# Hybrid attention and expert block: values as weights in two column halves, result kept turned

## The reference

```python
xn = rms_norm(h, attn_norm_w)
q_a, k_a, v_a, q_b, k_b, v_b, g_a, g_b = split(xn @ w_in)
# y_a: sliding window (128), 8 heads of 64 over 2 key heads, QK-norm, ALiBi, a sink per head
probs = softmax(concat([scores, sink]))[..., :-1];  y_a = probs @ v_a
# y_b: stick-breaking, 8 heads of 64, strictly causal
between = cumsum(log_keep, reverse=True) - log_keep
weights = where(strict, exp(log_beta + between), 0);  y_b = weights @ v_b
merged = sigmoid(g_a) * (y_a @ w_proj_swa) + sigmoid(g_b) * (y_b @ w_proj_sb)
h = h + merged @ w_out
h = h + moe_ffn(rms_norm(h, ffn_norm_w), ...)       # top 4 of 32 experts
```

## Time and profile before

| | us |
|---|---|
| median of three timed runs | 2426.76 |
| lowest, highest | 2422.87, 2428.86 |
| the profiled execution | 2425.16 |
| its span, first to last instruction | 2423.4 |
| TensorE busy | 2283.3 |
| VectorE busy | 1584.5 |
| ScalarE busy | 1348.1 |
| GpSimd busy | 635.0 |

### The profile page before, as it was taken

The page is one execution under the profiler, slowest core; times in us unless marked ns, Lnnn a source line. Parts: engine busy times, 40 slices in busy tenths (PEclk is TensorE's granted clock), DMA queues, the critical chain, the costliest instruction groups (busy, mean ns, idle before and its releaser), DMA issues.

```text
span 2423.4 us, 39427 instructions
## 1 busy us (share of the span) xinstructions
PE 2283.3 (94%) x14040; PEld 1790.2 (74%) x14041; DVE 1584.5 (65%) x1607; ACT 1348.1 (56%) x1524; POOL 635.0 (26%) x505
## 2 busy tenths in 40 slices
PE   6979999899988899699999999999999999999995
PEld 5858878787876778477777777777787777777774
DVE  4035474656524434578788778788898778777775
ACT  4147374655634421356667666576776566565664
POOL 3611101010101110313454443133333123122222
PEclk9989999999998999799999999999999999999998
DMA  5000211112224442599899999899999889888984
GB/s 159 31 26 23 66 38 43 52 34 62 59 64 160 144 165 96 225 353 335 284 343 335 319 314 354 286 350 335 353 396 344 284 280 354 288 276 291 316 310 140
DMA packets 272998, 526.29 MB, mean 217 GB/s; under 512 B 33953, under 2 KB 82140, under 8 KB 272764
## 3 DMA queue, kind: packets, MB, share of 16 engines
q1 hardware_dynamic: 244316, 477.80, 54.7%
q0 software_dynamic: 17088, 43.30, 7.7%
q10 hardware_dynamic: 11520, 4.20, 0.7%
HBM read 481.07 MB, written 48.35 MB: 218 GB/s over the span
## 4 chain that ended last, share of the span: by engine, by line
PE 56%; DVE 1%; ACT 1%; issue 0%; DMA 0%; POOL 0%; POOLq 0%; ACTq 0%; DVEq 0%
PE ex_gu L1973 28%; PE ex_yp L2021 14%; PE ex_rest L1995 5%; PE ex_rest L2038 3%; PE ex_gu L1964 1%; PE ex_gu L1931 1%; PE ex_tr L1939 1%; PE ex_gu L1939 1%; PE ex_yp L2010 1%; DVE ex_wlo L1850 0%; ACT ex_whi L1596 0%; PE ex_rest L1989 0%; PE ex_gu L1947 0%; PE ex_tr L1931 0%; DMA ex_xg<-xn_s,ex_idx 0%
## 5 line engine op out<-in xcount | busy, mean ns | idle before, releaser
L1850 DVE TENSOR_TENSOR ex_wlo<-ex_raw,ex_whi 128x2048 fp32r<-128x2048 f32 x387 | 876.1, 2290 | 205.9 <-ACT ex_whi L1596 195.6
L1596 ACT ACTIVATE ex_whi<-ex_raw 128x2048 fp32r<-128x2048 f32 x387 | 735.1, 1926 | 211.3 <-PE ex_gu L1973 153.4
L1973 PE MATMUL ex_gu<-ex_whi,ex_xhi 128*128 128x512 f32 x1024 | 290.3, 405 | 2.4 <-ACT ex_whi L1596 2.4
L1973 PE MATMUL ex_gu<-ex_whi,ex_xlo 128*128 128x512 f32 x1024 | 275.1, 390 | 0.0
L1973 PE MATMUL ex_gu<-ex_wlo,ex_xhi 128*128 128x512 f32 x1024 | 273.8, 389 | 0.0
L1973 PEld LDWEIGHTS ex_gu<-ex_whi,ex_xhi 128*128 128x128 f32 x1024 | 191.5, 188 | 53.7 <-issue 10.2
L1973 PEld LDWEIGHTS ex_gu<-ex_whi,ex_xlo 128*128 128x128 f32 x1024 | 192.8, 188 | 41.6
L1973 PEld LDWEIGHTS ex_gu<-ex_wlo,ex_xhi 128*128 128x128 f32 x1024 | 192.2, 188 | 40.5
L665 POOL TENSOR_TENSOR at_wlo<-at_raw,at_whi 128x1024 fp32r<-128x1024 f32 x32 | 77.7, 2429 | 506.3 <-ACT at_whi L500 506.3
L57 PE MATMUL at_job<-xnT_hi,at_whi 128*128 128x512 f32 x448 | 190.6, 425 | 0.0
L59 PE MATMUL at_job<-xnT_hi,at_wlo 128*128 128x512 f32 x448 | 176.6, 394 | 0.0
(11 more groups left out here) (298 smaller groups left out, 3921.1 us busy)
## 6 DMA issues: line engine op xcount, KB each, us to landing
ex_raw<-in_w_gate_up_dram SPq DMA_DIRECT2D x512, 512.0 KB, 9.4
ex_raw<-in_w_down_dram SPq DMA_DIRECT2D x256, 512.0 KB
at_raw<-in_w_in_dram SPq DMA_DIRECT2D x28, 512.0 KB
gT<-at_gst SPq DMA_DIRECT2D x32, 256.0 KB, 2.2
mg_g<-gT SPq DMA_DIRECT2D x32, 256.0 KB, 3.0
n_x<-in_x_dram SPq DMA_DIRECT2D x8, 512.0 KB, 8.2
ring<-y_s SPq DMA_DIRECT2D x16, 256.0 KB, 4.5
raw_o<-in_w_out_dram SPq DMA_DIRECT2D x8, 512.0 KB, 6.1
```

What stands on the lines that cost most here:

```text
L1596: nc.scalar.activation(w_hi[:, i % RING, :], raw[:, i % SLABS, :], ACT.Copy).then_inc(hi_d, 1)
L1850: nc.vector.tensor_tensor(w_lo[:, slot, :], raw[:, i % SLABS, :], w_hi[:, slot, :].bitcast(F32), ALU.subtract).then_inc(lo_d, 1)
L1973: mm = nc.tensor.matmul(gu[:, half, h, :], x[:, k, :], w[:, kk, h, :], start=k == 0 and n == 0, stop=k == KD - 1 and n == 2)
```

## The change

1. `weigh`: the values of a head (128 keys x 64) are the weights, and the turned probabilities (128 columns) stream. Head 0 of the pair writes partitions 0 to 63 of `yT`, head 1 partitions 64 to 127, so the result comes out turned. For single heads one `weigh` after the odd unit does both heads. There are 16 such calls a pair instead of 20 (`WEIGHED`, `result_of`).
2. The division by the window's denominators moves from the result to the probabilities: `denominators` ends with a multiply of `prob`, stands in the body of the unit before, behind its preparations, and `turn` of a window unit waits for it.
3. The order on TensorE within a body: scores, values of unit n - 1, transposes, projections; for window units all transposes come after the early quarters. On ScalarE, `a2(n + 1)` goes ahead of `evac_tr` in window units.
4. `QUARTERS` lists the quarters of each unit, unit 19 included.
5. The first tiles come as qb, kb, qa, ka. Scores of units 0 and 1 follow job 4; jobs 4 to 7 use the banks `job`, `tr`, `job`, `pv`; their norms stand between the preparations of units 0 and 1.
6. y is stored as (2, 512, tokens). The merge loads eight pieces of 128 x 1024 straight, without transposes, behind its first tile's weights, and multiplies for the first tile as each piece is split.

```diff
+QUARTERS = [2, 2, 4, 4, 2, 2, 4, 4, 4, 4, 2, 2, 2, 2, 4, 2, 2, 4, 2, 2]
...
@@ ScalarE
+                before = last_reader(NU * p + u)
+                if before >= 0:
+                    act.wait_ge(pv_mm, result_of(before) + 3)
...
+                if UNITS[u][0] == "swa":
+                    a2(n + 1)
+                    evac_tr(p, u, (0,))
+                    if ahead:
+                        a1(ahead[0], 1)
...
+            finish_first(4, first_bank[4])
+            a1(0, 0)
+            a1(0, 1)
+            first_norm(0)
+            a1(1, 0)
+            a1(1, 1)
+            finish_first(5, first_bank[5])
+            a2(0)
+            first_norm(1)
+            finish_first(6, first_bank[6])
             split_hi(len(PAIR_TILES))
+            first_norm(2)
+            finish_first(7, first_bank[7])
@@ VectorE
                 nc.vector.reciprocal(stat["rden"][:, s, :], stat["den"][:, s, :]).then_inc(n_st, 1)
+                dve.wait_ge(n_st, 3 * w + 2)
+                mine = bsl(prob, u)
+                rden = stat["rden"][:, s, :].rearrange("p (a o) -> p a o", o=1).to_broadcast(list(mine.shape))
+                nc.vector.tensor_tensor(mine, mine, rden, ALU.mult).then_inc(n_st, 1)
...
             def body(n):
                 p, u = divmod(n, NU)
-                if UNITS[u][0] == "swa":
-                    denominators(p, u)
-                if n:
+                if weighed(n - 1):
                     result(*divmod(n - 1, NU))
                 for m in taken_up(n):
                     prepare(m)
                 for jl in ends_in(u - 1) if u else []:
                     if norm_of(p, jl) is not None:
                         finish_norm(p, jl)
+                if u + 1 < NU and UNITS[u + 1][0] == "swa":
+                    denominators(p, u + 1)
@@ TensorE
-                pe.wait_ge(a2_done, NU * p + u + 3)
+                if kind == "sb":
+                    pe.wait_ge(a2_done, NU * p + u + 3)
+                else:
+                    pe.wait_ge(n_st, 3 * (NSWA * p + u - NSB) + 3)
...
+                for m in range(blocks):
+                    for h in range(2):
+                        kb = tiles[m][1]
+                        turned_h = probT[:, h, m, :] if len(heads) == 1 else probT[:, slot(u), h * blocks + m, :]
                         v = vb[:, kb, bass.ds(P * p + HD * h, HD)] if kind == "sb" else va[:, kb, bass.ds(HD * p, HD)]
-                        last = nc.tensor.matmul(pv[:, hs * HD:(hs + 1) * HD], probT[:, slot(u), n, :], v,
-                                                start=m == 0, stop=m == len(mine) - 1)
+                        last = nc.tensor.matmul(yT[h * HD:(h + 1) * HD, :], v, turned_h,
+                                                start=m == 0, stop=m == blocks - 1)
...
+            project(4, every, first_bank[4], 0)
             score(0)
+            sum_squares(0)
+            project(5, every, first_bank[5], 0)
+            project(6, every, first_bank[6], 6)
+            sum_squares(1)
+            project(7, every, first_bank[7], 0)
+            sum_squares(2)
@@ merge
+                for n in range(2 * KA4):
+                    a, k = divmod(n, KA4)
+                    after(sp, ylo, n - 3)
+                    sp.dma_start(yraw[:, n % 4, :], y_s[a, k * P:(k + 1) * P, :]).then_inc(y_in[n % 4], 16)
...
+                pe.wait_ge(wlo_d, 3)
+                for a in range(2):
+                    for k in range(KA4):
+                        pe.wait_ge(ylo, KA4 * a + k + 1)
+                        for half in range(2):
+                            last = split3(nc, acc[:, 2 * half + a, :], w_hi[:, 0, a, k, :], w_lo[:, 0, a, k, :],
```

More of the change, by code:

```diff
@@ L296, with result_of, weighed, last_reader @@
 NG = sum(GROUPS)
+WEIGHED = [len(heads) == 2 or heads[0] == 1 for _, _, heads in UNITS]
+NR = sum(WEIGHED)
+def result_of(n):
+    p, u = divmod(n, NU)
+    return NR * p + sum(WEIGHED[:u])
+def weighed(n):
+    return n >= 0 and WEIGHED[n % NU]
+def last_reader(n):
+    u = n % NU
+    return n - 1 if u == SINGLES or (0 < u < SINGLES and u % 2 == 0) else n - 2
 def turned(n):
@@ L307 @@
 PAIR_TILES = ["qa", "ka", "qb", "kb"]
+FIRST_TILES = ["qb", "kb", "qa", "ka"]
 GATES_A_PAIR = 3
@@ L324 @@
 NF = len(PAIR_TILES) + PAIRS * TILES_A_PAIR
+QUARTERS = [2, 2, 4, 4, 2, 2, 4, 4, 4, 4, 2, 2, 2, 2, 4, 2, 2, 4, 2, 2]
 def quarters_of(u):
[L329 to L333, removed]
+    first = sum(QUARTERS[:u])
+    return [divmod(q, 4) for q in range(first, first + QUARTERS[u])]
 def taken_up(n):
@@ L720, in promote @@
                     dve.wait_ge(nrm_d, 4 * p)
-                else:
-                    dve.wait_ge(job_ev, 5)
-                for n, kind in enumerate(("qa", "ka")):
+                for kind in kinds:
+                    n = ("qa", "ka").index(kind)
+                    if p == 0:
+                        dve.wait_ge(job_ev, 2 * n + 7)
                     nc.vector.tensor_copy(cur_hi[kind][:, :], nxt[kind][:, :]).then_inc(cur_d, 1)
@@ L822, in body @@
                     promote(p + 1)
-            for n in (0, 1):
-                prepare(n)
+            finish_first(4, first_bank[4])
+            prepare(0)
+            prepare(1)
+            for jl in (5, 6):
+                finish_first(jl, first_bank[jl])
+                if jl == 5:
+                    promote(0, ("qa",))
             for n in range(NU * PAIRS):
@@ L934, in body @@
                 early, late = mine[:len(mine) // 2], mine[len(mine) // 2:]
-                if n == 0:
-                    for jl, part in mine:
-                        project(first_job(p) + jl, (part,), job[:, :])
-                    early = late = []
-                score(n + 2)
-                turn(p, u, (0,))
-                if n:
-                    weigh(*divmod(n - 1, NU))
+                score(n + 2)
+                if n == 2:
+                    pe.wait_ge(job_ev, 9)
+                if weighed(n - 1):
+                    weigh(*divmod(n - 1, NU))
+                if n == 0:
+                    pe.wait_ge(job_ev, 7)
+                if UNITS[u][0] == "sb":
+                    turn(p, u, (0,))
+                if n == 0:
+                    sum_squares(3)
                 for jl in ends_in(u - 1) if u else []:
```

148 lines of the change are left out of this document (61 added, 87 removed).

## The result

| | before | after |
|---|---|---|
| median, us | 2426.76 | 2411.62 |
| lowest, highest | 2422.87, 2428.86 | 2411.27, 2414.06 |
| profiled execution, its span | 2425.16, 2423.4 | 2411.3, 2409.5 |
| TensorE busy, products | 2283.3, 14040 | 2237.9, 13880 |

The ratio of after to before is 0.9941, 95% interval 0.9928 to 0.9953: the profiled execution is 13.9 us shorter and the median 15.1, where 31 were forecast. The direction and the range held; less than half of the gain came.

What follows compares the result with a forecast made beforehand. TensorE bounds the pairs' long middles, chains of latencies the start and pair ends; -22 - 17 + 19 - 2.4 - 0.8 - 8 = -31 from 2425.16 gives 2394 us, range 2362 to 2420.

Steps and rivals of the forecast that it cites:

- Start: Up to the scores of unit 4: these start at 169.0 instead of 191.0, -22 us (bounds -14 and -25).
- Rival E: Start: it gives only half because new banks and waits line up badly; 2405 us, chance 0.09.
- Value passes: Products with the values: 0.054 us a pass plus 0.19 a visit, saving 5.5 us in a pair's middle.
- the middle: Units 2 to 17 of each pair, bound by TensorE: net 4.3 us saved a pair, -17 for four.
- rival D: Value passes: the halves do not overlap with 64-column loads, so slower than before; 2433 to 2438 us, chance 0.10.
- Rival C: Window units: VectorE's spare is gone, each of some 20 short units runs 1 us longer; 2414 us, chance 0.16.
- Pair ends: Unit 19's transposes wait for VectorE's division behind two preparations: +6.3 us at each of three ends, +19.
- Rival B: Pair ends: the added wait is met on time and costs nothing; 2375 us, chance 0.15.
- Units 0 and 1: Stretch after each pair end, still a chain: -0.8 us each, -2.4 in all (bounds -6 and +6).
- Merge: After attention: transposes go, first tile ends 13.5 us earlier, 5 to 6 given back: -8 us (bounds -2 and -12).
- then a wait for GpSimd: Merge, sign of being right: first tile done within 2 us of the last low part, then TensorE waits for GpSimd.
- Later stages: Output projection, routing and experts: they keep their instructions and were costed at nothing.

Runs made afterwards that it cites:

- the later first scores: Changed kernel with the first pair's scores behind job 5 instead of job 4: 2417.01 us, 0.9960.
- The heads in turn: Changed kernel with the value products' loops exchanged, all blocks of head 0, then all of head 1: 2430.95 us, 1.0014.
- the division between: Changed kernel with unit 19's division between VectorE's two preparations, and ScalarE's Exp and Ln ahead of `a2` and the evacuation: 2396.59 us, 0.9875.
- the weights ahead: Merge's tile weights loaded two tiles ahead: 2397.61 us, 0.9879 in the changed kernel; 2414.43 us, 0.9946 in the kernel before.
- the repeats: Both kernels run again without edit: kernel before 2428.09 us, 0.9999; changed kernel 2412.81 us, 0.9934.
- the half pieces: Changed kernel with the merge's result loaded in 16 pieces of 128 x 512 instead of eight of 128 x 1024: 2415.75 us, 0.9948.
- its eight versions: The changed kernel with further edits, one run for each of eight follow-up experiments: from 2381.35 us to 2430.95 us.

## Why the prediction was right where it was, and wrong

**Start: right.** The scores of unit 4 came at 170.0 for a forecast of 169.0. The stages were as told: no wait of TensorE from the first scores to the second, then a chain of 14.8 us for a forecast of 14.9 + 0.7. The second scores came at 155.25, 1.8 us later than the 153.4 of the sum (whose terms add up to 153.5), behind two waits that it did not have: 0.9 us more for GpSimd's low part and 0.9 ahead of the first scores. The shorter chain hid 0.8 of that. The clock of 0.62 that the prediction calls "about half way between the two levels" is a quarter of the way from 0.5 to 1.0; no term hangs on it. Rival E, a start worth half, is out with 21.0 us. That the new waits cost little held with this order only, as the later first scores show.

**Value passes: right; the middle: a wait put at nothing.** A visit of 32 passes took 1.90 us, where 32 x 0.054 + 0.19 gives 1.92. All passes of units 2 to 17 took 11.8 us after 17.1, by their starts: -5.3 for a forecast of -5.5. The heads in turn exclude rival D. The Trainium skill (TensorEngine Tiling, Key Properties) says that a change of the tiling mode drains the array. Taken as a whole record's length at each end, as the prediction tried it, such a visit would take 32 x 0.054 + 0.56 = 2.29 us; the visit took 1.90, so the trace shows a price of about 0.2 us for both ends together.

The step that failed here is in the prediction's sum for the middle. It lets the saved pass time and the moved quarters cost no waiting in the middle ("respreading costs no cycles"), and its only charge is "0.15 x 8 = 1.2". The projections of a middle grew by 2.1 us, 70.8 to 73.0 from their starts to the next instruction's, and 1.2 of these are a wait ahead of unit 5's transposes, for ScalarE's copy of the last turned probabilities of unit 4, which frees their bank. The rows stand in the third pair, TensorE, then ScalarE:

```profile
477.80 0.40 PE L59 MATMUL at_job<-xnT_hi,at_wlo 128*128 128x512 f32 x1
479.40 0.63 PE L953 MATMUL at_tr<-ident,at_prob 128*128 128x128 f32 x4 [1.21 <-ACT at_probT L610]
```

```profile
478.89 0.36 ACT L610 ACTIVATE at_probT<-at_tr 128x256 f32<-128x256 f32 x1
```

That copy stands on ScalarE behind other work without a gap. All four pairs have the wait (1.21, 1.21, 1.21 and 0.83 us); the first three have one more, 1.11, 0.47 and 0.47 us, for ScalarE's squares. What is left of the projections' growth, 0.9 us, is within the charge. So a middle gave 2.6 to 3.3 us and not 4.3, and the last with its end 3.5 where 5.1 was due: 5.3 us of the miss. Rival C, window units bound by VectorE, is out: no wait over 0.25 us stands in the middle's window units, and TensorE is busy in 103.66 of 105.97 us.

**Pair ends: right**, in size (+6.3, +6.2, +6.3 for +6.3 each), place and releaser. The stand was 9.76 us, VectorE's first preparation started 5.6 us behind the scores as forecast, and the next scores came 19.8 us behind them. Rival B, that these ends cost nothing, was not the kernel's; the division between shows what such a kernel is worth, 15 us.

**Units 0 and 1: nearly.** -1.1 for -2.4. In one of the three the mean clock was 0.92, where 0.98 and 1.00 were granted in the others, and it took 15.1 us instead of 14.2 and 14.0.

**Merge: the largest step that failed.** Counted from the end of attention (721.3 before, 705.4 after), "the second tile at 748.6" is 27.3 us; it came at 32.8, and 36.7 was the kernel before. These 5.5 us are the miss. The forecast had the high copy of the second tile's weights start 1.3 us sooner than in the kernel before, at 24.0 us, "with it out of the way"; it started at 27.9 (733.34). Of these 3.9 us, 1.3 are the table load, which still stands there, and some 2.7 are the weights' landing: "the same bytes" did not land at the same pace, with SyncE waiting for room. The last piece's low part, placed at 743 (21.7 us behind the end of attention), ended at 24.8 (730.15), as late. The other 1.6 us lie behind the copy: a second table load of 1.28 us, the sigmoid of the gates (735.70) and the product that frees the banks (736.79). TensorE waited for these, not for GpSimd's low part, which ended at 736.82; the item of my list "then a wait for GpSimd" was wrong. The first tile ended 2.5 us after the last low part (732.62 and 730.15), where I gave 2. Two later tiles inherit a landing in the same way, as the gap of 4.04 us at 765.88 shows, but the kernel before has such gaps too. That the four-piece room is what delayed the landing is read from SyncE's waits; no run with more room was made. With the weights ahead the changed kernel gains 14 us and the kernel before 13, and the merge's share of the change rises only from 2.2 to 4.3 us: late weights explain about 2 of the 5.8 us that the merge lacks of its 8, and the rest stays.

**Later stages: costed at nothing, +4.3.** The instructions of the output stage and the experts are the same, and they are 2.1 and 2.2 us longer in the profiled run. In the output stage the two families of kernels overlap (146.6 to 149.8 us over the changed kernel and its versions, 147.4 to 148.4 over the kernel before and its own), so only a part of its 2.1 us can be laid to the change. In the experts they don't: 1427.9 to 1429.6 against 1426.2 to 1427.0. Nearly all of it arises where the first expert's products start. Windows of before, then of after, both from the first product with the expert's weights on:

```profile
1012.90:1018.90 6.00, 6.00 (x20) 4.88 (x21) 6.00 (x3) 5.35 (x4) 5.79 (x4) 0.74 1.05 407
1018.90:1024.90 6.00, 6.00 (x52) 4.01 (x51) 6.00 (x4) 3.75 (x2) 5.57 (x3) 1.00 1.05 408
```

```profile
997.10:1003.10 6.00, 5.47 (x12) 3.89 (x13) 6.00 (x3) 5.28 (x3) 5.79 (x4) 0.50 1.04 404
1003.10:1009.10 6.00, 5.84 (x47) 3.92 (x48) 5.41 (x4) 3.84 (x2) 5.37 (x4) 0.88 1.06 406
```

DMA moves as much in both. What differs is TensorE: in after it stands 0.51 us more ahead of the fourth product, for which the profile names no releaser, and its granted clock is 0.50 over the first 6 us, the level of 1.2 GHz, where the kernel before had 0.74. Sixteen products in, it is 2.8 us behind by their starts, and this distance stays until 0.6 us of it go at the very end. TensorE had stood idle alike ahead of both (10.5 and 10.9 us, then 2.41). What brings the short stand, and whether it is what keeps the clock down, is open. Scatter is excluded by the repeats, and the form of the merge's loads by the half pieces; nothing else was tried.

## What to carry to other kernels

Where two narrow products can share the array, alternate them pass by pass between the column halves; in long runs the gain hangs on that order, and in visits of eight passes it made no difference here. Work that gets shorter on the busiest engine arrives sooner at its next wait: look at each wait that was met just in time. A wait that is added to one engine should be priced by all that stands ahead of its releaser on that engine's queue, and then bought back by moving the releaser between, not ahead of, those items. When a stage's start moves up, follow the next tile's loads, with the room that their issues wait for, and the instruction that frees its PSUM banks before counting on it: here half of the shift was worth anything, and weights loaded one tile sooner were worth nearly as much as the whole change.

## What the runs showed that I had not expected

- The granted clock behind a stretch in which TensorE is busy 10 to 11 of 14 to 15 us is not the same in every execution of the same code: 1.00 or 0.61 over the next 4 us, which makes units 2 and 3 18.5 or 20.1 us long, and moved the end of attention by 4 us between two executions. A difference of this size between two single runs says nothing by itself.
- Passes with 64 weight columns and 128 streamed take 0.059 us each when the halves alternate, 0.102 when long runs keep to one half, and about 0.074 in visits of eight in either order (0.59 us).
- The first expert depends by 2 us on something upstream that changes no instruction of it: the granted clock over its first 6 us is 0.50 to 0.52 in the changed kernel, its repeat and its eight versions, and 0.74, 0.65 and 0.68 in the kernel before, its repeat and its version with the weights ahead.
